# Unscaled softmax queries: the norm factor of a query goes into the exponential's scale

## The reference

```python
q = q_groups(rope(rms_norm(split_heads(q, N_HEADS), q_gain), positions), g)
s = jnp.einsum('bgrqd,bgkd->bgrqk', qb, kb).astype(jnp.float32) * SCALE
```

```python
m = jnp.maximum(jnp.max(s, axis=-1, keepdims=True), sink)
e = jnp.exp(s - m)
return e / (jnp.sum(e, axis=-1, keepdims=True) + jnp.exp(sink - m))
```

## Time and profile before

| what | value |
|---|---|
| median of 3 runs (lowest, highest) | 899.0 us (898.86, 900.75) |
| the profiled execution's own time | 900.66 us |
| its span, first to last instruction | 898.8 us |
| PE busy | 828.0 us (92%) |
| DVE busy | 555.2 us (62%) |
| ACT busy | 425.1 us (47%) |
| POOL busy | 122.0 us (14%) |
| mean granted TensorE clock | 0.964 |

### The profile page before, as it was taken

How to read it: one execution, slowest core, us unless ns; L and a number is a source line. 1 busy time by engine, 2 the same in 40 slices (tenths; PEclk the granted TensorE clock), 3 DMA queues, 4 the chain that set the end, 5 groups by cost and what they waited for, 6 DMA issues and landing times.

```text
span 898.8 us, 13794 instructions
## 1 busy us (share of the span) xinstructions
PE 828.0 (92%) x5394; PEld 730.7 (81%) x5394; DVE 555.2 (62%) x948; ACT 425.1 (47%) x824; POOL 122.0 (14%) x130
## 2 busy tenths in 40 slices
PE   5989889998977899998899999999999899999997
PEld 4768787776877678998788868887998688999996
DVE  5898666646966745344645536776675664555555
ACT  4435637735444644434534524455343534444443
POOL 2335004511711300000010110021000100000000
PEclk9999889999969999999899999999999999999999
DMA  9746121033523135452342332322555365565551
GB/s 313 192 152 204 67 94 48 2 110 114 184 94 96 61 102 170 158 187 94 99 137 94 95 109 89 131 94 94 165 187 187 108 219 171 190 210 189 166 178 47
DMA packets 93504, 121.48 MB, mean 135 GB/s; under 512 B 8760, under 2 KB 69616, under 8 KB 93440
## 3 DMA queue, kind: packets, MB, share of 16 engines
q1 hardware_dynamic: 92432, 117.80, 40.5%
q0 software_dynamic: 432, 1.57, 0.5%
q10 hardware_dynamic: 576, 1.23, 0.4%
HBM read 119.55 MB, written 1.05 MB: 134 GB/s over the span
## 4 chain that ended last, share of the span: by engine, by line
PE 73%; DVE 14%; ACT 5%; issue 4%; POOL 1%; POOLq 0%; DVEq 0%; ACTq 0%
PE bank L406 20%; PE bank L408 19%; PE bank L407 19%; DVE w_lo L1301 4%; PE bank L534 2%; PE bank L581 2%; ACT w_hi L963 1%; PE bank L548 1%; PE bank L528 1%; ACT tmp L1061 1%; PE bank L835 1%; PE bank L413 1%; PE bank L412 1%; DVE small L1390 1%; DVE xres L1472 1%
## 5 line engine op out<-in xcount | busy, mean ns | idle before, releaser
L1301 DVE TENSOR_TENSOR w_lo<-raw,w_hi 128x1024 fp32r<-128x1024 f32 x216 | 268.0, 1247 | 162.0 <-ACT w_hi L963 159.9
L963 ACT CAST w_hi<-raw 128x1024 fp32r<-128x1024 f32 (+1 forms) x217 | 226.0, 1044 | 176.1 <-PE bank L408 167.2
L406 PE MATMUL bank<-h_hi,w_hi 128*128 128x256 f32 (+1 forms) x800 | 235.2, 294 | 7.6 <-DVE ar L1684 3.7
L407 PE MATMUL bank<-h_lo,w_hi 128*128 128x256 f32 (+1 forms) x800 | 231.4, 289 | 0.0
L408 PE MATMUL bank<-h_hi,w_lo 128*128 128x256 f32 (+1 forms) x800 | 230.4, 288 | 0.0
L406 PEld LDWEIGHTS bank<-h_hi,w_hi 128*128 128x128 f32 x800 | 155.9, 195 | 12.3 <-DVE ar L1684 4.0
L407 PEld LDWEIGHTS bank<-h_lo,w_hi 128*128 128x128 f32 x800 | 156.4, 195 | 0.3
L408 PEld LDWEIGHTS bank<-h_hi,w_lo 128*128 128x128 f32 x800 | 156.3, 195 | 0.0
L406 PE MATMUL bank<-w_hi,h_hi 128*128 128x512 f32 (+1 forms) x288 | 116.0, 403 | 12.8 <-DVE w_lo L1301 6.3
L408 PE MATMUL bank<-w_hi,h_lo 128*128 128x512 f32 (+1 forms) x288 | 113.5, 394 | 0.0
L407 PE MATMUL bank<-w_lo,h_hi 128*128 128x512 f32 (+1 forms) x288 | 113.4, 394 | 0.0
(11 more groups left out here) (313 smaller groups left out, 1240.6 us busy)
## 6 DMA issues: line engine op xcount, KB each, us to landing
raw<-in_w_in SPq DMA_DIRECT2D x24, 1024.0 KB, 5.2
raw<-in_a_w_in SPq DMA_DIRECT2D x14, 1024.0 KB, 5.2
raw<-in_w_ffn_gate SPq DMA_DIRECT2D x11, 1024.0 KB, 5.3
raw<-in_w_ffn_up SPq DMA_DIRECT2D x11, 1024.0 KB, 5.3
raw<-in_w_ffn_down SPq DMA_DIRECT2D x11, 1024.0 KB, 5.0
raw<-in_b_w_in SPq DMA_DIRECT2D x9, 1024.0 KB, 5.3
raw<-in_w_gate SPq DMA_DIRECT2D x8, 1024.0 KB, 5.3
raw<-in_a_w_out SPq DMA_DIRECT2D x4, 1024.0 KB, 5.0
```

Of the source, the lines that this page charges most:

```text
L406: mm(o, lh, rh, start=start, stop=False)
L407: mm(o, lh, rl, start=False, stop=False)
L963: nc.scalar.copy(split(w_hi, s), rawsub(s)[0]).then_inc(S["hi_ready"], 1)
L1301: V.tensor_tensor(split(w_lo, s), rawsub(s)[0], split(w_hi, s).bitcast(F), ALU.subtract).then_inc(S["lo_ready"], 1)
```

## The change

The queries are left unscaled by their norm. GpSimd only makes their power, into a new tile `rq` (token tile by head), and multiplies keys alone. The factor is positive, so the maximum of a row of scores is the maximum of the unscaled row times it: DVE multiplies the column of negated maxima by `rq`, and the exponential takes `rq` as its scale. In the compressed branch the 128x512 tile of scores is multiplied as a whole, since one exponential does all rows. The transposes of queries wait for `rp_raw` in place of `rp_out`, and in phase 1 they get six banks of their own (6, 7, 2, 3, 4, 5), with waits on `rp_free` before each pair.

The diff, cut; a second parameter of `tbank` is passed in `q_hi`, `key_hi`, `q_lo` and `key_lo` alike:

```diff
+        rq = sm[:, 604:636].rearrange("p (t h) -> p t h", t=2)
...
-        def tbank(e):
-            return ps[(6, 7, 4, 5)[e % 4]]
+        def tbank(e, phase=0):
+            return ps[(6, 7, 2, 3, 4, 5)[e]] if phase else ps[(6, 7, 4, 5)[e % 4]]
...
-                    elif e >= 4:
-                        pe.wait_ge(S["tq_dve"], 8 + e - 3 if phase else e - 7)
+                    elif phase == 0 and e >= 8:
+                        pe.wait_ge(S["tq_dve"], e - 7)
...
             pe.wait_ge(S["rp_free"], 10)
-            pe.wait_ge(S["rp_out"], 4)
+            pe.wait_ge(S["rp_raw"], 4)
             head_transposes(2, 0, k_tiles(1, 4) + q_tiles(0) + q_tiles(1))
...
             z_tiles(0, za, 2, 3)
-            pe.wait_ge(S["rp_out"], 8)
+            pe.wait_ge(S["rp_out"], 4)
...
             z_tiles(1, first["b_z"], 0, 2)
-            pe.wait_ge(S["rp_out"], 12)
+            pe.wait_ge(S["rp_raw"], 11)
             head_transposes(0, 1, q_tiles(0))
-            pe.wait_ge(S["rp_out"], 14)
+            pe.wait_ge(S["rp_raw"], 12)
+            pe.wait_ge(S["rp_free"], 14)
             head_transposes(2, 1, q_tiles(1))
             z_tiles(1, first["b_z"], 2, 3)
+            pe.wait_ge(S["rp_free"], 16)
+            pe.wait_ge(S["rp_out"], 6)
             head_transposes(4, 1, k_tiles(2, 2))
...
                         for i in range(4 // (qt + 1)):
-                            A(t[:, w * i:w * i + w], b[:, w * i:w * i + w], ACT.Exp, bias=nmax[:, c + i:c + i + 1], accum_out=sums[:, c + i:c + i + 1])\
+                            h = heads[i // len(brs)]
+                            A(t[:, w * i:w * i + w], b[:, w * i:w * i + w], ACT.Exp, bias=nmax[:, c + i:c + i + 1], scale=rq[:, qt, h:h + 1],
+                              accum_out=sums[:, c + i:c + i + 1])\
...
                     last = V.tensor_reduce(m, ps[2 + j % 2][:, :].rearrange("p (r n) -> p r n", r=nb), X, ALU.max, negate=True)
+                    h = heads[0]
+                    link(last)
+                    mv = m.rearrange("p (h b) -> p h b", b=len(brs))
+                    last = V.tensor_tensor(mv, mv, bc(rq[:, qt, h:h + nb // len(brs)], [P, nb // len(brs), len(brs)], 2), ALU.mult)
...
             pcv = pc.rearrange("p (h c) -> p h c", c=16)
+            link(V.tensor_tensor(pcv, pcv, bc(sm[:, 604:636], [P, 32, 16], 2), ALU.mult))
             link(V.tensor_reduce(cmx, pcv, X, ALU.max))
...
-            def head_rstd(i, heads, out):
-
-                if i:
-                    pool.wait_ge(S["rp_out"], i)
+            def query_rstd(i):
+
+                rstd(rq[:, i % 2, 8 * (i % 4 // 2):8 * (i % 4 // 2) + 8], rp_va[:, 0:8], "rp_sum", i + 1, "rp_rstd")
+
+            def key_rstd(i, n, heads, out):
+
+                if n:
+                    pool.wait_ge(S["rp_out"], n)
                 rstd(rp_rs[:, 0:heads], rp_va[:, 0:heads], "rp_sum", i + 1, "rp_rstd")
...
-            for i in range(8):
-                head_rstd(i, 8 if i < 4 else 4, q8(i % 2, i // 2) if i < 4 else kd[i // 2][:, i % 2])
+            for i in range(4):
+                query_rstd(i)
+            for i in range(4):
+                key_rstd(4 + i, i, 4, kd[2 + i // 2][:, i % 2])
...
-            for i in range(6):
-                head_rstd(8 + i, 8 if i < 4 else 2, q8(i % 2, i // 2) if i < 4 else kd[2][:, i % 2, 0:2])
+            for i in range(8, 12):
+                query_rstd(i)
+            for i in range(2):
+                key_rstd(12 + i, 4 + i, 2, kd[2][:, i, 0:2])
```

More of the change, by code:

```diff
@@ L495, in head_transposes @@
                         pe.wait_ge(S["tq_c"], e - 3)
-                    elif e >= 4:
-                        pe.wait_ge(S["tq_dve"], 8 + e - 3 if phase else e - 7)
+                    elif phase == 0 and e >= 8:
+                        pe.wait_ge(S["tq_dve"], e - 7)
                     for j, t in enumerate(src):
-                        last = nc.tensor.transpose(tbank(e)[:, P * j:P * j + P], t, ident)
+                        last = nc.tensor.transpose(tbank(e, phase)[:, P * j:P * j + P], t, ident)
                     last.then_inc(S["tq_ps"], 1)
@@ L1020, in q_hi @@
                 act.wait_ge(S["tq_ps"], base + e + 1)
-                b = tbank(e)[:, :].rearrange("p (a n) -> p a n", a=4)
+                b = tbank(e, base > 0)[:, :].rearrange("p (a n) -> p a n", a=4)
                 for u, (lo, inc) in enumerate(((0, "act"), (64, "tq_hi"))):
@@ L1026, in key_hi @@
                 act.wait_ge(S["tq_ps"], base + e + 1)
-                b = tbank(e)[:, 0:P * groups].rearrange("p (a n) -> p a n", a=groups)
+                b = tbank(e, base > 0)[:, 0:P * groups].rearrange("p (a n) -> p a n", a=groups)
                 nc.scalar.copy(k_hi[:, 0:groups, br, P * tt:P * tt + P], b).then_inc(S["tq_hi"], 1)
@@ L1357, in key_lo @@
                 dve.wait_ge(S["tq_hi"], hi_at + 1)
-                b = tbank(e)[:, 0:P * groups].rearrange("p (a n) -> p a n", a=groups)
+                b = tbank(e, e < 8)[:, 0:P * groups].rearrange("p (a n) -> p a n", a=groups)
                 V.tensor_tensor(k_lo[:, 0:groups, br, P * tt:P * tt + P], b, k_hi[:, 0:groups, br, P * tt:P * tt + P].bitcast(F), ALU.subtract)\
@@ L1390, in maxima @@
                     last = V.tensor_reduce(m, ps[2 + j % 2][:, :].rearrange("p (r n) -> p r n", r=nb), X, ALU.max, negate=True)
+                    h = heads[0]
+                    link(last)
+                    mv = m.rearrange("p (h b) -> p h b", b=len(brs))
+                    last = V.tensor_tensor(mv, mv, bc(rq[:, qt, h:h + nb // len(brs)], [P, nb // len(brs), len(brs)], 2), ALU.mult)
                     if phase:
-                        h = heads[0]
                         link(last)
```

## The result

Twenty timed runs of each kernel gave 899.93 us before and 901.71 after: a ratio of 1.0022 (95% interval 1.0014 to 1.0030), so 1.3 to 2.7 us slower. One execution of the kernel before, at 1022.87 us, was far slower than the rest and is not in the ratio. A second set of runs gave 1.0012 (1.0001 to 1.0023). On the 899.0 us shown ahead of the prediction the first ratio is 901.0. Forecast were 899.1 us, a range of 895.3 to 902.3 and "no difference" as the likeliest case. The range holds the result; it lies just past the 0.2% line, on the slower side.

What follows compares the result with a forecast made beforehand. VectorE bounds phase 0's query preparation, PE its settled jobs, a VectorE-ACT chain most other touched parts. Gains of 6.3 us (5.0 + 1.3) against losses of 6.45 (2.05 + 1.0 + 0.2 + 3.2) gave 899.1 us, range 895.3 to 902.3.

Steps and rivals of the forecast that it cites:

- no difference: Whole kernel: time within 0.2% of before, 897.2 to 900.8 us; chance 0.47.
- VectorE's collisions with GpSimd: Query preparation, phase 0: without GpSimd's multiplies beside VectorE's `w_lo` and table operation, PE starts 3.3 us earlier.
- The clock stays up if 0.7 us of the wait are left: 58 to 63 us: PE's 2.70 us wait shrinks to about 0.7, the lower clock does not come, gaining 1.7 us.
- Start of phase 0: First jobs of phase 0, up to PE at 137.13: compressed multiply, three maxima and eight exponentials add 2.05 us.
- Settled jobs: Settled part of phase 0: 0.11 us a round over seven rounds plus VectorE's extra work, 1.0 us lost (0 to 2.5).
- Rival 2: Jobs of phase 0: ACT becomes the bound, losing 3.2 us in place of 1.0, 901.3 us; chance 0.22.
- sign of error: Settled part of phase 0: new PE waits for ACT above 0.2 us a round would show the prediction wrong.
- Heads of phase 1: Query preparation in phase 1: four GpSimd multiplies go, VectorE's chain up to the meta transposes moves 1.3 us earlier.
- the banks bring nothing by themselves: Phase 1 query transposes: own banks end PE's 4.01 us wait for GpSimd, but PE at 259.91 again waits for VectorE.
- Jobs of phase 1: Phase 1 chain: eight maxima add 1.6 us, 16 exponentials 1.45, the last 0.1; 3.2 us lost.
- rival 1: Additions hide or are cheaper, 896 us; or PE's clock returns sooner after its phase 1 wait, similar gain; chance 0.28.
- Slower by over 0.2%: Whole kernel: time over 900.8 us; chance 0.25.

Runs made afterwards that it cites:

- deferred kernel: Kernel before, but GpSimd multiplies phase 0's four query items only after the last key item, nothing added to the jobs: ratio 0.9923, second set 0.9950.
- additions alone: Kernel before, GpSimd multiplies kept, plus scale pointer and products on maxima and compressed tile, by a column of ones: ratio 1.0061, 5.5 us slower.
- products alone: Kernel before plus only VectorE's multiplies by ones, on the negated maxima and the compressed tile; exponentials as before: ratio 1.0035, 3.1 us slower.
- removal alone: Changed kernel without scale on the exponentials or multiplies on maxima and compressed tile, so the query norm is left out: ratio 0.9944, 5.0 us faster.
- scale alone: Kernel before plus only a column of ones as scale pointer of the 96 exponentials: ratio 0.9996 (0.9983 to 1.0008).
- deferred kernel of phase 1: Kernel before with GpSimd's query multiplies put off behind the key items in both phases: ratio 0.9968, 2.9 us faster than before.

## Why the prediction was right, and where it was off

- **VectorE's collisions with GpSimd: right.** 3.3 us forecast for the start of PE's panel, 57.45 to 54.04, 3.4 measured; with the clock's 1.7 us, 5.0 forecast and 5.0 measured. The deferred kernel keeps the multiplies and has the same gain, so it is their moment that counts.
- **The clock stays up if 0.7 us of the wait are left: right.** 0.54 us were left.
- **Start of phase 0, 2.05 us: measured 1.7** (from -5.0 to -3.3 in the table of landmarks, and 1.7 again with the additions alone: 139.0 for job 4 against 137.13, of which 0.15 is there at the gates). Taken singly, and less the 0.5 us that is there at the gates, the scale costs 0.4 us where 0.72 was forecast and the products 0.9 where 1.32 was; their sum is 0.4 below what both cost together.
- **Settled jobs, 1.0 us: measured 1.3**: 0.11 a round as worked out, and two longer steps, 0.33 and 0.32, to the scores of jobs 14 and 20. The products alone have both of these (0.26 and 0.27) and nothing else; why there is open. Rival 2 was this step made larger; it needed 0.4 us a round. The sign of error named for it, new waits of PE for ACT of more than 0.2 us a round, depends on the row: the weight loads wait 2.4 us more over the seven rounds, 0.3 a round, but PE itself stands idle for 0.76 us in all, 0.1 a round.
- **Heads of phase 1, 1.3 us: right** where nothing else changes (1.3 in the removal alone). That the banks bring nothing by themselves also holds: PE now waits 6.03 us for VectorE in one piece where it had waited 4.01 and 2.37, as its timeline after shows:

```profile
257.80 1.03 PE L723 MATMUL bank<-cst,ar 16*128 16x16 f32 x8 [6.03 <-DVE o_lo L1365]
```

- **Jobs of phase 1, 3.2 us: the size right, the way to it in part luck.** From the second scores to the last it is 36.76 us before and 39.59 after, 2.8 more; up to there the forecast's steps give 1.4 for seven maxima and 1.45 for the exponentials. But 1.4 of the 2.8 come in one step, from the scores of job 4 to those of job 5: 7.93 us after, 6.56 before. There the granted clock falls in the changed kernel and does not before:

```profile
276.99:284.92 7.93, 6.37 (x42) 5.83 (x43) 4.86 (x11) 4.64 (x11) 1.04 (x1) 0.78 0.40 132
```

What PE did ahead of it is also different. It waits 1.47 us for ACT before the scores of job 4, and 1.55 once more behind them; before, the first of the two is 0.52 us:

```profile
276.99 0.39 PE L529 MATMUL bank<-msk,crr 128*128 128x256 f32 x1 [1.47 <-ACT tmp L1066]
```

```profile
279.25 0.39 PE L528 MATMUL bank<-msk,crr 128*128 128x256 f32 x1 [0.52 <-ACT tmp L1061]
```

The step takes 7.9 to 9.4 us in the three profiles of the changed kernel and 8.1 with the products or both additions on ones, but 6.6 in both profiles of before, with the removal alone and with the scale alone. The forecast had no such fall of the clock. Without this step the additions cost 1.5 us, where the forecast's serial steps outside it give 2.0 to 2.5 (an estimate: 2.85 less one or two maxima and two to four exponentials in it, 0.4 to 0.8). So probably not all of them lie on the chain.
- **What the sum left out: the clock after PE's other waits.** From job 4 to job 6 of phase 0 the changed kernel took 7.0 us and not 6.1, and in the first z tile of phase 1 5.1 and not 6.2, which is the second way in which rival 1 could come about. The two nearly cancel, and before has both values too: 6.1 and 7.4, 6.2 and 5.2 in its two profiles.
- **The result itself** is 1.0 to 1.9 us above the forecast. The step that failed is the last, from the profile's sum to the median of the runs: 0.15 us in the profiled stretch became 1.1 to 2.0 in the timed runs. "Slower by over 0.2%" had 0.25 and "no difference" 0.47; the likeliest was missed by a hair in one set, and met in the other.

## What to carry to other kernels

When a helper engine's work slows a full one, first try to move it to where the full one has room; spreading the same work over the hot loop cost more here than the collision did (0.20 us for each dependent small step, 0.09 for each pointer of an exponential, times the jobs that lie on the chain). Where it is moved to, look at what the full engine does there: in phase 0 the four multiplies met idle time, in phase 1 they held one small operation of VectorE for 3.8 us and lost more than they gained. Before adding to a loop that is bound elsewhere, measure its room: additions that each fit may not fit together. And a profile of one execution can be off by 3 us in code that nobody changed, so compare landmarks around the change, not spans.

## What was unexpected of the hardware

The moment at which TensorE's clock comes back after a wait differs between executions of the same kernel. Before the scores of job 4 of phase 0 PE has waited 2.27 and 1.48 us in both profiles of the kernel before. From these scores to those of job 6, with the same work:

```profile
137.13:143.25 6.12, 6.12 (x38) 5.05 (x38) 3.88 (x11) 3.98 (x12) 2.08 (x2) 0.74 0.43 138
```

```profile
137.42:144.82 7.40, 7.40 (x39) 5.81 (x39) 3.88 (x11) 3.98 (x12) 2.08 (x2) 0.59 0.44 142
```

A mix of 1.2 and 2.4 GHz in both, PE busy throughout, and 1.3 us between them. In the first z tile of phase 1 the two stand the other way round, 6.2 us at 0.54 and 5.2 at 0.67, though there the wait before it differs as well (2.37 and 3.50 us). Together with the 0.87 to 1.00 in 627 to 646 us this is as large as the whole effect of the change.

A GpSimd instruction can hold even a tiny VectorE operation until its own end. The scaling of two elements a partition takes 0.69 us in place of 0.17 and ends at 244.90; the multiply beside it ends at 244.88:

```profile
242.86 2.02 POOL L1911 TENSOR_TENSOR ar<-ar,small 128x512 f32<-128x512 f32 x1 [0.41 <-DVE ar L1343]
```

The 4.52 us of the meta tokens' multiply, in place of 0.74, is the largest case. GpSimd's own 128x512 multiply takes 2.02 us beside a `w_lo`, while four in a row in the deferred kernel of phase 1 take 4.03, a microsecond each.
